# One mixer's helper work in another order: weight splits, scores and the recurrence's parts of a float32 transformer kernel

## The reference, cut to what matters

```python
def even_mixer(hn, w_in, conv_w, conv_b, ga_w, ga_b, gx_w, gx_b, lam, f_b, w_out):
    proj = hn @ w_in                                  # 1024 x 2568
    xr, yr, q, k, v, f_logit = jnp.split(proj, EVEN_SPLITS, axis=-1)
    xc = causal_depthwise_conv(xr, conv_w, conv_b)    # 4 taps
    h_lru = rglru(xc, ga_w, ga_b, gx_w, gx_b, lam)    # gates, recurrence over time
    y_a = (h_lru * jax.nn.gelu(yr.astype(jnp.float32))).astype(hn.dtype)
    log_f = jax.nn.log_sigmoid((f_logit + f_b).astype(jnp.float32))
    y_b = fox_attention(q.reshape(shp), k.reshape(shp), v.reshape(shp), log_f)  # 8 heads of 64
    return jnp.concatenate([y_a, y_b], axis=-1) @ w_out

def rglru(x, ga_w, ga_b, gx_w, gx_b, lam):
    r = jax.nn.sigmoid(block_diag_linear(xf, ga_w, ga_b))
    i = jax.nn.sigmoid(block_diag_linear(xf, gx_w, gx_b))
    log_a = -LRU_C * r * jax.nn.softplus(-lam)
    a = jnp.exp(log_a)
    u = jnp.sqrt(-jnp.expm1(2.0 * log_a)) * (i * xf)
    # h[t] = a[t] * h[t-1] + u[t]
```

## Time and profile before

| What | Value |
|---|---|
| median of three runs | 2541.49 us |
| the profiled execution | 2540.97 us, its span 2539.3 us |
| TensorE matmul busy | 2480.6 us, 98% |
| VectorE, ScalarE, GpSimdE busy | 80%, 60%, 3% |
| the chain that ended last | TensorE 93%, VectorE 4%, ScalarE 2%, issue 1% |
| mean TensorE clock granted | 0.994 |

### The profile page before, as it was taken

The page is one execution under the profiler, slowest core; times in us unless marked ns, Lnnn a source line. Parts: engine busy times, 40 slices in busy tenths (PEclk is TensorE's granted clock), DMA queues, the critical chain, the costliest instruction groups (busy, mean ns, idle before and its releaser), DMA issues.

```text
span 2539.3 us, 39706 instructions
## 1 busy us (share of the span) xinstructions
PE 2480.6 (98%) x14390; PEld 2115.8 (83%) x14390; DVE 2029.1 (80%) x2919; ACT 1535.1 (60%) x2127; POOL 68.4 (3%) x152
## 2 busy tenths in 40 slices
PE   9999999899999999999999999999999999999998
PEld 8788887788888888888888788888888888897887
DVE  6677764789899989999999877778877877787776
ACT  6554453577777777777777754453544644634543
POOL 8000000000000000000000000000000000000000
PEclk9999999999999999999999999999999999999999
DMA  7356643499999999999999966632566566423663
GB/s 213 113 175 186 184 144 124 149 370 369 356 359 372 363 358 359 368 369 353 362 380 361 345 190 192 183 92 93 176 190 189 172 190 186 139 85 109 191 194 103
DMA packets 481900, 597.33 MB, mean 235 GB/s; under 512 B 21882, under 2 KB 313154, under 8 KB 481760
## 3 DMA queue, kind: packets, MB, share of 16 engines
q1 hardware_dynamic: 478048, 589.47, 69.5%
q0 software_dynamic: 3712, 6.00, 0.9%
HBM read 594.35 MB, written 1.05 MB: 234 GB/s over the span
## 4 chain that ended last, share of the span: by engine, by line
PE 93%; DVE 4%; ACT 2%; issue 1%; DMA 0%; ACTq 0%; DVEq 0%
PE bank L811 24%; PE bank L617 15%; PE bank L837 12%; PE bank L653 12%; PE bank L623 8%; PE bank L602 6%; PE bank L599 2%; PE bank L1456 1%; PE bank L873 1%; PE bank L822 1%; PE bank L979 1%; PE bank L1150 1%; PE bank L758 1%; PE bank L1289 0%; PE bank L633 0%
## 5 line engine op out<-in xcount | busy, mean ns | idle before, releaser
L2102 DVE TENSOR_TENSOR wlo_ring<-raw_ring,whi_ring 128x1024 fp32r<-128x1024 f32 (+1 forms) x1122 | 1328.1, 1220 | 129.7 <-ACT whi_ring L1506 112.5
L1506 ACT CAST whi_ring<-raw_ring 128x1024 fp32r<-128x1024 f32 (+1 forms) x1122 | 1144.2, 1052 | 164.6 <-DMA raw_ring<-in_od_exp_w_dram 152.7
L617 PE MATMUL bank<-x,whi_ring 128*128 128x512 f32 x1720 | 428.3, 391 | 0.0
L617 PEld LDWEIGHTS bank<-x,whi_ring 128*128 128x128 f32 x1720 | 315.6, 188 | 60.7
L623 PEld LDWEIGHTS bank<-x,wlo_ring 128*128 128x128 f32 x1720 | 220.9, 191 | 8.4
L623 PE MATMUL bank<-x,wlo_ring 128*128 128x256 f32 x1720 | 223.5, 283 | 0.0
L1570 ACT COPY arena<-bank 128x256 f32<-128x256 f32 x110 | 40.9, 372 | 283.9 <-PE bank L623 283.9
L602 PE MATMUL bank<-x,whi_ring 128*128 128x256 f32 (+2 forms) x1024 | 192.7, 289 | 0.9 <-DVE x L2172 0.9
L811 PE MATMUL bank<-whi_ring,xg0hi 128*128 128x512 f32 x448 | 177.7, 397 | 0.2 <-issue 0.2
L811 PE MATMUL bank<-whi_ring,xg1hi 128*128 128x512 f32 x448 | 177.2, 395 | 0.0
L811 PE MATMUL bank<-whi_ring,xg0lo 128*128 128x512 f32 x448 | 174.8, 390 | 0.0
(11 more groups left out here) (514 smaller groups left out, 3460.9 us busy)
## 6 DMA issues: line engine op xcount, KB each, us to landing
raw_ring<-in_od_exp_w_dram SPq DMA_DIRECT2D x672, 512.0 KB, 5.5
raw_ring<-in_ffn_w_gate_dram SPq DMA_DIRECT2D x88, 512.0 KB, 4.0
raw_ring<-in_ffn_w_up_dram SPq DMA_DIRECT2D x88, 512.0 KB, 5.0
raw_ring<-in_ffn_w_down_dram SPq DMA_DIRECT2D x88, 512.0 KB, 3.5
raw_ring<-in_ev_ffn_w_dram SPq DMA_DIRECT2D x66, 512.0 KB, 3.9
raw_ring<-in_w_in_dram SPq DMA_DIRECT2D x42, 512.0 KB, 4.1
raw_ring<-in_od_w_in_dram SPq DMA_DIRECT2D x24, 512.0 KB, 3.9
raw_ring<-in_ev_w_in_dram SPq DMA_DIRECT2D x20, 512.0 KB, 7.0
```

The costliest lines, as they stand in the source:

```text
L617: mm_ = mm(bank[:, :], wh[:, kt, :], X2[:, kt, :, :].rearrange("p a n -> p (a n)"), start=(start and kt == 0), stop=(stop and kt == KT - 1 ...
L1506: nc.scalar.copy(WHI[:, slot, 0:n], RAW[:, slot, 0:n]).then_inc(s["hi_ready"], 1)
L2102: V_.tensor_tensor(WLO[:, slot, 0:n], RAW[:, slot, 0:n], WHI[:, slot, 0:n].bitcast(F32), ALU.subtract)\
```

## The change

It leaves the work as it is, but for one buffer, and moves instructions on three engines:

1. ScalarE converts chunk 2, besides 0 and 1, before it scales the first activations. VectorE makes the low part of chunk 0 alone before the activations' low parts; that of chunk 1 follows them.
2. Both gates are counted once, after all 16 matmuls, and ScalarE waits for that before its first sigmoid.
3. VectorE makes the low parts of chunks 12 to 15 between the convolution's passes, 16 and 17 before the input product, 18 before the squares, 19 and 20 before the first logits.
4. The squares go into the buffer `RG` instead of `XR`.
5. TensorE computes unit 13 before the first two scores, and waits for the constants' columns ahead of these scores instead of ahead of the first transposition.
6. ScalarE evicts unit 13 and converts chunk 20 right after the root, before the first exponentials.
7. The recurrence's first high part moves from round 7 to the head of round 8, its second to fourth behind the exponential of round 8. The first low part stands at the end of round 7 and the others in round 8.

```diff
--- before.py
+++ after.py
@@ -957,13 +957,14 @@
                     for i in range(4):
                         last = mm(BANK[b + i // 2][:, (i % 2) * S:(i % 2 + 1) * S], w[:, i, :], XC[:, i, :],
                                   start=True, stop=True)
-                    last.then_inc(s["gates_mm"], 1)
+                last.then_inc(s["gates_mm"], 1)
                 for k in range(10, 13):
                     u(k)
                 pe.wait_ge(s["loads_done"], 16 * N_LOADS)
                 pe.wait_ge(s["consts_ready"], 2)
                 pe.wait_ge(s["sig_ready"], 8)
                 turn_columns(1, 3)
+                u(13)
 
                 x_at = nxt("x_ready", KT) - KT
 
@@ -1022,14 +1023,12 @@
                         last.then_inc(s["recx_mm"], 1)
 
                 pe.wait_ge(s["cumev_ready"], 1)
+                pe.wait_ge(s["cols_ready"], 2)
                 scores(0)
                 scores(1)
-                u(13)
                 for v in range(16):
                     if v < 8:
                         u(14 + v // 2, v % 2 * KT // 2, (v % 2 + 1) * KT // 2)
-                        if v == 0:
-                            pe.wait_ge(s["cols_ready"], 2)
                     else:
                         if v == 8:
                             pe.wait_ge(s["probt_copied"], 8)
@@ -1747,8 +1746,8 @@
                 for i in range(4):
                     ahead(c0 + 9 + i)
                     evict(6 + i, YR[:, i, :], ACT.Gelu_apprx_tanh)
-                for n, (g, name, b) in enumerate(((RG, "ga_b", 4), (IG, "gx_b", 6))):
-                    act.wait_ge(s["gates_mm"], n + 1)
+                act.wait_ge(s["gates_mm"], 1)
+                for g, name, b in ((RG, "ga_b", 4), (IG, "gx_b", 6)):
                     for i in range(4):
                         af(g[:, i, :], BANK[b + i // 2][:, (i % 2) * S:(i % 2 + 1) * S], ACT.Sigmoid,
                            bias=col(name, i)).then_inc(s["sig_ready"], 1)
@@ -1766,6 +1765,8 @@
                 ahead(c0 + 16)
                 act.wait_ge(s["root_in"], 1)
                 af(TH[:, :, :], TH[:, :, :], ACT.Sqrt).then_inc(s["root_ready"], 1)
+                evict(13, K[:, 1, :], ACT.Copy)
+                ahead(c0 + 17)
 
                 def hi(kt, src):
                     nc.scalar.copy(XHI[:, kt, :], src).then_inc(s["evhi_ready"], 1)
@@ -1787,8 +1788,6 @@
 
                 exps(0)
                 exps(1)
-                evict(13, K[:, 1, :], ACT.Copy)
-                ahead(c0 + 17)
                 for v in range(16):
                     if v < 8 and v % 2:
                         ahead(c0 + 17 + v // 2)
@@ -1797,19 +1796,17 @@
                             evict(u, Q[:, u // 2 - 5, :], ACT.Copy, 64 ** -0.5)
                         else:
                             evict(u, K[:, u // 2 - 5, :], ACT.Copy)
-                    if v == 7:
-                        act.wait_ge(s["chunk_used"], c0 + 21)
+                    if v == 8:
                         act.wait_ge(s["lru_ready"], 1)
                         hi(0, YR[:, 0, :])
                     copy(v)
-                    if v == 7:
-                        hi(1, YR[:, 1, :])
                     if v + 2 < 16:
                         exps(v + 2)
                     if v == 7:
-                        for kt in (2, 3):
+                        act.wait_ge(s["chunk_used"], c0 + 21)
+                    if v == 8:
+                        for kt in range(1, 4):
                             hi(kt, YR[:, kt, :])
-                    if v == 8:
                         ahead(oc)
                     if v == 9:
                         ahead(oc + 1)
@@ -2051,7 +2048,7 @@
             for t in range(TT):
                 act.wait_ge(x_loaded[t], 16)
                 mean_square(t)
-            ahead(-2)
+            ahead(-1)
             act.wait_ge(s["first_ready"], 1)
             gain("norm_mix0")
             even_mixer(EV_PROJ, EV_OUT)
@@ -2459,8 +2456,7 @@
                 evict(5, XR[:, 3, 4:S + 4])
                 dve.wait_ge(s["bank_free"], q0 + 6)
                 for j in range(4):
-                    if j == 2:
-                        ahead(c0 + 9)
+                    ahead(c0 + 9 + j)
                     for i in range(4):
                         x = XR[:, i, 1 + j:1 + j + S]
                         w = col("conv_w", 4 * j + i)
@@ -2477,23 +2473,22 @@
                 V_.tensor_copy(CC[:, :, :], BANK[3][:, 0:16].rearrange("p (t h) -> p t h", t=TT))\
                     .then_inc(s["cumev_ready"], 1)
                 dve.wait_ge(s["cumev_ready"], 1)
-                squares = flat_(XR)[:, 0:4 * S]
-                for j in range(3):
-                    ahead(c0 + 10 + j)
+                ahead(c0 + 14)
                 dve.wait_ge(s["sig_ready"], 8)
                 link(V_.tensor_tensor(flat_(IG), flat_(IG), flat_(XC), ALU.mult))
-                ahead(c0 + 13)
+                ahead(c0 + 15)
                 dve.wait_ge(s["aexp_ready"], 4)
-                link(V_.tensor_tensor(squares, flat_(AE), flat_(AE), ALU.mult))
-                ahead(c0 + 14)
+                link(V_.tensor_tensor(flat_(RG), flat_(AE), flat_(AE), ALU.mult))
                 dve.wait_ge(s["cols_tp"], 2)
                 for t in (1, 2):
                     last = V_.tensor_copy(COLS[:, t, :], BANK[6 - t][:, 0:P])
                 last.then_inc(s["cols_ready"], 1)
                 dve.wait_ge(s["cols_ready"], 2)
                 dve.wait_ge(s["aexp_ready"], 8)
-                V_.scalar_tensor_tensor(flat_(TH), squares, 1.0, flat_(TH), ALU.add, ALU.mult)\
+                V_.scalar_tensor_tensor(flat_(TH), flat_(RG), 1.0, flat_(TH), ALU.add, ALU.mult)\
                     .then_inc(s["root_in"], 1)
+                ahead(c0 + 16)
+                ahead(c0 + 17)
 
                 def logits(v):
                     h, t = v // 2, v % 2
@@ -2522,13 +2517,9 @@
 
                 logits(0)
                 logits(1)
-                for j in range(3):
-                    ahead(c0 + 15 + j)
                 for v in range(16):
                     if v in (5, 9, 13):
                         scaled(v // 4 - 1)
-                    if v == 7:
-                        lo(0, YR[:, 0, :])
                     if v + 2 < 16:
                         logits(v + 2)
                     if v % 4 == 3:
@@ -2547,9 +2538,9 @@
                     if v < 8 and v % 2:
                         ahead(c0 + 17 + v // 2)
                     if v == 7:
-                        lo(1, YR[:, 1, :])
+                        lo(0, YR[:, 0, :])
                     if v == 8:
-                        for kt in (2, 3):
+                        for kt in range(1, 4):
                             lo(kt, YR[:, kt, :])
                         ahead(oc)
                     if v == 9:
@@ -3054,7 +3045,7 @@
                 dve.wait_ge(x_loaded[t], 16)
             norm()
             dve.wait_ge(s["first_ready"], 1)
-            ahead(1 - LEAD)
+            ahead(-LEAD)
             gain("norm_mix0")
             even_mixer(EV_PROJ, EV_OUT)
             residual(EV_OUT)
```

## The result

The changed kernel took 2556.0 us (median of 4 runs, 2553.1 to 2557.8) where the kernel before took 2541.2 (4 runs): 14.8 us between the medians. Thirteen executions of the changed kernel are on record, 2552.8 to 2565.8 us with a median of 2556.7 and a mean of 2557.9; the ratio, 1.0067 with a 95% interval of 1.0048 to 1.0088, fits their mean and says about 17 us slower (12 to 22). The forecast was 2553.3, with a range up to 2556.5: the median of the four runs lies just inside, the median of the thirteen and the ratio (2558.5) outside. The direction and the places were right, the amount too small. Five further runs beside the kernel before (the eighth experiment) gave 2562.4 us and 1.0082 [1.0069, 1.0095].

The account below looks back on a forecast made before the run. TensorE, busy 98% of the span, was taken as the bound, with 0.2 us to gain in the mixer. Terms 1.45 + 2.15 + 2.5 + 2.2 + 2.3 + 1.25 = 11.85 us gave 2553.3 us, range 2548.5 to 2556.5.

Parts of the forecast that it names:

- 1 start: Ahead of the second unit: chunk 2's earlier cast and chunk 1's later low part delay TensorE 1.45 us (0.9 to 2.9).
- 2 convolution: Ahead of the gates: four low parts between VectorE's passes make TensorE stand 2.15 us (1.0 to 2.5).
- 3 scores: Behind unit 13: TensorE waits 2.5 us (1.5 to 3.0) for the second column copy ahead of the scores.
- 4 first transposition: Ahead of the first transposition of probabilities: a 2.4 us wait (1.7 to 2.8), 2.2 after taking off the old 0.2.
- 5 recurrence: Ahead of the first two output projection blocks: later parts cost 2.3 us (1.8 to 2.5) and 1.25 (0.5 to 1.5).
- clock: TensorE's clock in the mixer's new gaps: the forecast added nothing for falls.
- The clock's rival: TensorE's clock falls in the mixer's new gaps, 1.7 us each: one fall makes 2555.0, two 2556.7; chance 0.25.
- the trace's gap at 1459: Behind the mixer, a 2.73 us gap followed at once by clock 1.00, taken as grounds for adding nothing.

Follow-up runs that it names:

- the eighth experiment: The changed kernel run again unaltered, beside the kernel before: 2562.4 us, ratio 1.0082.
- the eleventh: The changed kernel with its five gaps filled by unread products, unit-form ahead of gates, scores and first transposition, identity ahead of two output blocks: 2551.9 us, ratio 1.0041.
- the twelfth: The kernel before with the gates' two halves counted once, after all sixteen products, nothing else changed: 2544.4 us, ratio 1.0016.
- Third: The kernel before with only the recurrence's high and low parts moved one round later: 2547.4 us, ratio 1.0020.
- the fourth: The changed kernel with 35 small unread matmuls put into TensorE's five new gaps: 2553.7 us, ratio 1.0041.
- the ninth: The kernel before with only the changed order between gates and second softmax round, plus 9 identity products ahead of scores and 9 ahead of first transposition: 2545.6 us, 1.0018.
- tenth: The kernel before with only the changed order between gates and second softmax round, plus 18 and 16 unit-form products ahead of scores and first transposition: 2545.6 us, 1.0017.
- the sixth kernel: The changed kernel with the recurrence's high and low parts put back in their old rounds: 2549.9 us, ratio 1.0039.
- first: The kernel before with only the start's order changed (chunk 2 converted early, chunk 1's low part later): 2542.1 us, ratio 1.0003.
- second: The kernel before with only the four low parts put between the convolution's passes: 2543.2 us, ratio 1.0003.

## Why the forecast was too small

By its own steps, with the gaps as the profiles of the changed kernel (C) and of the filled or single kernels show them:

| term | forecast | measured |
|---|---|---|
| 1 start | 1.45 | 1.14 (C), 0.9 to 1.2 alone |
| 2 convolution | 2.15 | 2.93 - 1.14 = 1.8 (C), 1.8 alone |
| 3 scores | 2.5 | 2.42 (C) |
| 4 first transposition | 2.2 | 0.79 - 0.2 = 0.6 (C, slowed ahead of it), 2.3 - 0.2 = 2.1 filled |
| 5 recurrence | 2.3 + 1.25 | 2.29 + 1.12 (C) |
| clock | 0 (rival: 1.7 a fall) | 4.4 (C); in the runs 10.8, if the eighth (+21.2) is set against the eleventh (+10.4) |

**The start** was read right in mechanism. The data of chunk 2 came a little earlier than the estimate from 384 GB/s: its cast stands at 9.97 (landing estimated at 10.1), the gain at 10.94 (11.15), so the activations were 0.4 late, not 0.6. **The convolution** differs by the passes: I took 2.10 for the first and 1.88 for the other three from the earlier trace rows. But 1.88 is the second pass alone: in the same trace the third and fourth, behind a low part, took 3.44 us together (L2470 x8 from 44.81), 1.72 each. In the new order all took less:

```profile
42.03 1.57 DVE L2464 TENSOR_SCALAR arena<-arena,cols 128x256 f32<-128x256 f32 x4
45.33 1.23 DVE L2099 TENSOR_TENSOR wlo_ring<-raw_ring,whi_ring 128x1024 fp32r<-128x1024 f32 x1 [1.73 <-ACT whi_ring L1505]
46.47 1.67 DVE L2466 SCALAR_TENSOR_TENSOR arena<-arena,cols 128x256 f32<-128x256 f32 x4
```

The low parts between them waited for the casts, as replayed, so only the last pass's 0.2 and some 0.15 ahead of it came through: 0.36 in all (forecast start of the gates, moved by the start's 1.14: 54.41; measured 54.05). **The scores and the transposition's chain** came out link by link, each 0.4 to 0.5 early, most of it that same 0.36: the scores at 71.88 for 71.15 + 1.14 = 72.29, the first transposition at 77.76 for 77.15 + 1.14 = 78.29. **The recurrence** came within 0.15.

What the gaps are worth without a fall, the filled kernels say: the eleventh 2551.9 against 2541.5, 10.4 us (one short fall in its profile included), and the parts alone 0.86 + 1.78 + 4.45 + 3.45 = 10.5, where the forecast had 11.85. So the gaps' terms were together over 1 us too long, and this hid a part of the missing clock term: the forecast's distance from the result is smaller than the term it left out.

**What failed is the sentence "by the trace's gap at 1459 nothing is added, and I take nothing".** The clock term, put at nothing, measured 4.4 us in the first profile and 13.2 in the eighth's. The clock's rival had the mechanism, and its chance and its price were wrong. The chance, 0.25, was judged on two gaps, one with a fall (421) and one without (1459). Behind the mixer the same trace has four more of 2.0 to 2.6 us, at 429, 1452, 1767 and 2303, all followed by full clock. For the first of them (in a row by stretch the granted clock is third from the end):

```profile
429.07 0.70 PE L1150 MATMUL bank<-whi_ring,x 128*128 128x512 f32 x2 [2.61 <-DVE x L2673]
...
430.00:432.00 2.00, 2.00 (x11) 1.62 (x10) 2.00 (x4) 1.87 (x2) 0.00 (x0) 1.00 0.00 0
```

One in six, then; but four of the forecast's own gaps were 2 us and longer, and at one in six each the chance of at least one fall is 1 - (5/6)^4 = 0.52, an estimate. What no row of the kernel before could say is how these places would fare: half clock followed the scores' bare gap in four profiles of four and the first output block's in three of three. Nor was the gap at 1459 an exception, as the profiles taken later show. It kept its 2.7 us in eight of the fourteen, and half clock followed in two; here in the twelfth's:

```profile
1462.36 1.09 PE L899 MATMUL bank<-ident,h 128*128 128x128 f32 x8 [2.73 <-DVE h L3079]
...
1464.00:1466.00 2.00, 2.00 (x12) 0.50 0.00 0
```

The gap at 429 was followed by half clock in eight profiles of fourteen, those at 1767 and 2303 in four of fourteen each: together with the two of eight, 18 of 50 at these four places. So the length of a gap of 2.1 to 2.7 us doesn't settle whether half clock follows, and the same gap can have it in one execution and not in the next; why the two places of the mixer had it every time isn't shown.

The price was wrong too. It was read from one example: the 1.7 us came from a fall of 3.4 us, which is the shortest there was. Falls of 6.8 (twice), 10.2 and 23.9 us stood in the mixers, at 43% of their length each: 1.5 us for the shortest, 10.3 for the longest. The spread of the times goes with it. The 13 executions of the first comparison ranged from 2552.8 to 2565.8 us, with mean clocks of 0.992 down to 0.986, and 0.001 of mean clock is 2.5 us of 2550.

The Trainium skill, "TensorE: Matmul & The Clock Gate", section "What's actually happening", calls the throttled state the default that activity releases, and adds that the same kernel sees a different number of slow products at its start from run to run. By the first every new gap was at risk. The mixer's profiles agree for its gaps of 2.29 to 2.44 us (half clock behind 7 bare ones of 7), but the eighth's doesn't agree that activity releases the clock: it stayed at 0.50 for 22 us with TensorE busy in all of them. The second agrees in kind: the same five gaps gave one mixer 13.5 us longer and one 21.4.

The accounts close with this price. First profile: waits 1.14 + 1.8 + 2.42 + 0.6 + 2.29 + 1.12 = 9.4, three falls of 3.4 at 43% 4.4, together 13.8; measured 13.8 at the mixer's end and in the span. Eighth: waits 1.14 + 1.8 + 2.44 - 0.2 + 2.29 + 1.12 = 8.6, falls of 23.9, 3.4 and 3.4 us at 43% 13.2, together 21.8; measured 159.26 - 137.51 = 21.75. Third: 2.5 + 4.4 = 6.9; measured 7.2. (A few tenths of each fall lie in idle time, which the sums leave out.) These accounts are of the mixer alone. Behind it, where all kernels are alike, a profile can be off by its own falls: the time from the mixer's end to the end of the span was the same as before in the first profile, about 2.5 us longer in the fourth's and the eighth's, and 1.8 shorter in the ninth's and tenth's.

Open stay: why the same fall at the scores lasted 3.4 us in one execution and 23.9 in another of the same kernel; why the sixth kernel, which has the eighth's order up to the recurrence, shows no sign of such a long fall in its 5 runs (2547.4 to 2551.4, mean clock 0.992 or 0.993; one is profiled, with 6.8 us); and where the twelfth's falls stood.

## What to carry to other kernels

When a change opens a gap on an engine that was busy there, price the gap and the clock behind it apart: the first from the replay of the helpers, the second as a share of a fall (43% of it here) whose length can't be read from one example. Nor can its chance be read from one row: look at every gap of that size in the trace, and at the same gap in several executions. If reordering is needed all the same, products that nobody reads, put into the gap, can be cheaper than the gap: the changed kernel was 15 and 21 us slower than before with bare gaps, 12 and 10 with filled ones. And a wait behind a slowed stretch hides its true length; fill the earlier gap to see it.

## What was new of the hardware

- In the mixer gaps of 2.29 to 2.44 us on TensorE were followed by half clock (0.50) that lasted 3.4 to 23.9 us, up to 22 of them with the engine busy all the time; so were 18 of 50 gaps of 2.1 to 2.7 us at four places behind it. Gaps of 0.6, 1.5 and 1.2 us in the mixer (first, second, twelfth) weren't, in the profiles taken; one of 1.12 was, twice, 6 us behind one of 2.29.
- Half clock also came with no gap left over 0.4 us just ahead of it: in the fourth and eleventh kernels it began behind the scores, in units without a pause (eleventh, about 74.3 us, the last wait, 0.22 us, ended at 71.64). In the kernel before it began between 1700 and 1702 us (0.76), where the longest gap in the 40 us ahead was 1.26.
- VectorE's four-instruction passes took 1.57 and 1.67 us behind a low part in the changed kernel and 1.72 in the kernel before, and 2.10 and 1.88 in the earlier trace rows; what made them quicker wasn't tried.
